# Layer 0 begun tile by tile: rows, turns, copies and first products of a bidirectional encoder trunk

## The reference, cut to what matters

```python
def rms_norm(x, g):
    y = x32 * lax.rsqrt(jnp.mean(x32 * x32, axis=-1, keepdims=True) + NORM_EPS)
    return (y * g)

for l in range(DEPTH):                                   # DEPTH = 2
    h = rms_norm(x, attn_pre_norm[l])
    proj = jnp.einsum('bsd,dc->bsc', h, w_in[l])         # 1024 -> IN_COLS
    gates, mla_in, dil_in, diff_in = jnp.split(proj, SPLITS, axis=-1)
    ...                                                  # three attention mixers
    merged = g_mla * (o_mla @ w_branch_mla[l]) + g_dil * (o_dil @ w_branch_dil[l]) + g_diff * (o_diff @ w_branch_diff[l])
    x = x + rms_norm(merged @ w_out[l], attn_post_norm[l])
    h = rms_norm(x, ffn_pre_norm[l])
    x = x + rms_norm(conv_gated_mlp(h, w_up[l], ffn_conv[l], w_down[l]), ffn_post_norm[l])
```

## Time and profile before

| | us |
|---|---|
| median of 3 runs | 1029.82 |
| lowest and highest | 1029.73, 1029.85 |
| the profiled execution | 1029.86 |
| its span | 1028.1 |
| TensorE busy in it | 1013.2 (99%) |
| VectorE busy | 680.5 (66%) |
| ScalarE busy | 587.8 (57%) |

### The profile page before, as it was taken

How to read it: one execution, slowest core, us unless ns; L and a number is a source line. 1 busy time by engine, 2 the same in 40 slices (tenths; PEclk the granted TensorE clock), 3 DMA queues, 4 the chain that set the end, 5 groups by cost and what they waited for, 6 DMA issues and landing times.

```text
span 1028.1 us, 15935 instructions
## 1 busy us (share of the span) xinstructions
PE 1013.2 (99%) x6244; PEld 908.7 (88%) x6244; DVE 680.5 (66%) x932; ACT 587.8 (57%) x859; POOL 131.9 (13%) x257
## 2 busy tenths in 40 slices
PE   8999999999999999999999999999999999999997
PEld 7889999888888999999888899998888889999996
DVE  5635566655596887878865355666555869787877
ACT  5657666565446654555575666565653457455553
POOL 3353124000002000000024321230000020000000
PEclk9999999999999999999999999999999999999999
DMA  8555445454444555565564544465344645546551
GB/s 253 184 172 158 123 136 172 162 165 164 144 147 160 202 169 203 168 201 173 166 195 155 173 124 126 150 207 164 124 139 168 205 144 166 204 169 201 174 195 41
DMA packets 109038, 170.79 MB, mean 166 GB/s; under 512 B 3377, under 2 KB 72804, under 8 KB 108964
## 3 DMA queue, kind: packets, MB, share of 16 engines
q1 hardware_dynamic: 107676, 166.88, 50.0%
q10 hardware_dynamic: 1208, 2.63, 0.7%
q0 software_dynamic: 80, 0.26, 0.1%
HBM read 168.72 MB, written 1.05 MB: 165 GB/s over the span
## 4 chain that ended last, share of the span: by engine, by line
PE 96%; DVE 1%; ACT 1%; issue 1%; DVEq 0%; POOL 0%; POOLq 0%; ACTq 0%
PE bank L1418 28%; PE bank L1420 28%; PE bank L1419 28%; PE bank L1781 2%; PE bank L1682 1%; PE bank L1703 1%; PE bank L1774 1%; PE bank L1691 1%; PE bank L1719 1%; PE bank L1726 1%; PE bank L1771 1%; PE bank L1733 1%; PE bank L1739 1%; PE bank L1397 0%; DVE x_rows L1233 0%
## 5 line engine op out<-in xcount | busy, mean ns | idle before, releaser
L1053 DVE TENSOR_TENSOR w_lo<-w_raw,w_hi 128x2048 fp32r<-128x2048 f32 (+3 forms) x174 | 364.3, 2095 | 161.1 <-ACT w_hi L700 161.0
L700 ACT ACTIVATE w_hi<-w_raw 128x2048 fp32r<-128x2048 f32 (+3 forms) x174 | 304.7, 1752 | 50.6 <-PE bank L1420 48.9
L1418 PE MATMUL bank<-w_hi,hT_lo 128*128 128x512 f32 (+2 forms) x700 | 258.3, 369 | 2.1 <-DVE hT_lo L1127 1.3
L1420 PE MATMUL bank<-w_hi,hT_hi 128*128 128x512 f32 (+2 forms) x700 | 252.9, 361 | 0.0
L1419 PE MATMUL bank<-w_lo,hT_hi 128*128 128x512 f32 (+2 forms) x700 | 252.6, 361 | 0.0
L1418 PE MATMUL bank<-hT_hi,w_lo 128*128 128x256 f32 x704 | 199.4, 283 | 0.7 <-DVE hT_lo L1080 0.7
L1420 PE MATMUL bank<-hT_hi,w_hi 128*128 128x256 f32 x704 | 199.2, 283 | 0.0
L1419 PE MATMUL bank<-hT_lo,w_hi 128*128 128x256 f32 x704 | 199.2, 283 | 0.0
L1418 PEld LDWEIGHTS bank<-w_hi,hT_lo 128*128 128x128 f32 x700 | 131.5, 188 | 18.3 <-issue 3.5
L1420 PEld LDWEIGHTS bank<-w_hi,hT_hi 128*128 128x128 f32 x700 | 131.4, 188 | 14.0
L1419 PEld LDWEIGHTS bank<-w_lo,hT_hi 128*128 128x128 f32 x700 | 131.7, 188 | 13.0
(11 more groups left out here) (215 smaller groups left out, 1250.9 us busy)
## 6 DMA issues: line engine op xcount, KB each, us to landing
w_raw<-in_w_up_dram SPq DMA_DIRECT2D x44, 1024.0 KB, 4.9
w_raw<-in_w_in_dram SPq DMA_DIRECT2D x36, 1024.0 KB, 5.0
w_raw<-in_w_in_dram SPq DMA_DIRECT2D x36, 768.0 KB, 4.3
w_raw<-in_w_down_dram SPq DMA_DIRECT2D x22, 1024.0 KB, 4.8
w_raw<-in_w_out_dram SPq DMA_DIRECT2D x8, 1024.0 KB, 4.9
w_raw<-in_w_in_dram SPq DMA_DIRECT2D x8, 672.0 KB, 4.1
w_raw<-in_w_branch_mla_dram SPq DMA_DIRECT2D x4, 1024.0 KB, 4.9
w_raw<-in_w_branch_diff_dram SPq DMA_DIRECT2D x4, 1024.0 KB, 5.0
```

The source lines that it names most:

```text
L700: nc.scalar.activation(w_hi[:, n % RING, 0:nk * cols], raw[:, n % RING, 0:nk * cols], ACT.Copy).then_inc(hi_done, 1)
L1053: V.tensor_tensor(w_lo[:, n % RING, s], raw[:, n % RING, s], w_hi[:, n % RING, s].bitcast(F32), ALU.subtract).then_inc(lo_done, 1)
L1418: PE.matmul(dst, lhs[1], rhs_hi, start=start, stop=False)
L1420: return PE.matmul(dst, lhs[0], rhs_hi, start=False, stop=stop)
```

## The change

SP's first DMAs come in another order: the two row blocks of tile 0, piece 0, the two blocks of tile 1, piece 1, piece 2. `x_landed` becomes one semaphore per tile. TensorE's layer 0 goes through `begin` as layer 1 does, with a branch of its own: turn tile 0 when its rows are in, turn tile 1 when its rows are in, products of tile 0 with piece 0 (`first_part`, high weights first), tile 1 with piece 0, tile 0 with piece 1, tile 1 with piece 1. `use_first` and the layer-0 branches of `empty_turn` go. ScalarE has `start_hi`: four pairs of tile 0, high half of piece 0, two pairs of tile 1, high half of piece 1, two pairs of tile 1. VectorE has `start_lo` in the same order. The squares of the rows stay behind it.

```diff
--- before.py
+++ after.py
@@ -422,7 +422,7 @@
         conv_mid, conv_done = sem("conv_mid"), sem("conv_done")
         gelu_done, g_ready, g_hi_done, g_lo_done = sem("gelu_done"), sem("g_ready"), sem("g_hi_done"), sem("g_lo_done")
         gain_landed = sem("gain_landed")
-        x_landed = sem("x_landed")
+        x_landed = [sem(f"x_landed{t}") for t in range(NT)]
         positions_landed, parameters_landed, par_turned = sem("positions_landed"), sem("parameters_landed"), sem("par_turned")
         attn_gain_landed = sem("attn_gain_landed")
         lambda_landed = sem("lambda_landed")
@@ -529,9 +529,12 @@
         @block.sync
         def _(sp):
 
-            for t in range(NT):
+            def load_x(t):
+
                 for h in range(2):
-                    sp.dma_start(x[64 * h:64 * h + 64, t, :], tokens[h, :, t, :]).then_inc(x_landed, 16)
+                    sp.dma_start(x[64 * h:64 * h + 64, t, :], tokens[h, :, t, :]).then_inc(x_landed[t], 16)
+
+            load_x(0)
             for l in range(DEPTH):
                 for n, piece in enumerate(PIECES):
 
@@ -544,6 +547,8 @@
                         sp.dma_start(par_rows[:, 0:3 * DEPTH, :],
                                      a["ffn_conv"].rearrange("l t (c p) -> c (l t) p", p=P)).then_inc(parameters_landed, 16)
 
+                    if l == 0 and n == 1:
+                        load_x(1)
                     sp.sem_inc(slot_claimed, 1)
                     sp.dma_start(cut(raw, n), weight_source(l, *piece)).then_inc(raw_landed[n % RING], 16)
             store_rows(sp, 0)
@@ -782,16 +787,10 @@
 
             def empty_turn(l, what, banks=slice(None)):
 
-                if what == "attn" and l == 0:
-                    act.wait_ge(par_ready, 1)
                 if what == "latent" and l == 0:
                     act.wait_ge(par_ready, 2)
                 for b, (k0, nk) in list(enumerate(TURN_BANKS[what]))[banks]:
                     m = TURN_BEFORE[what] + TURN_STEP[what] * (b + 1)
-                    if what == "attn" and l == 0 and b == 1:
-                        split_hi(l, 0)
-                    if what == "attn" and l == 0 and b == 3:
-                        split_hi(l, 1)
                     act.wait_ge(turn_full, l * NTURN + m)
                     src = bank[4 + b]
                     if what == "merged":
@@ -822,6 +821,15 @@
                                                     scale=par_all[:, l, PRE_A + k:PRE_A + k + 1])
                     last.then_inc(turn_hi, 1)
 
+            def start_hi():
+
+                act.wait_ge(par_ready, 1)
+                begin_hi(0, 0, range(4))
+                split_hi(0, 0)
+                begin_hi(0, 1, (0, 1))
+                split_hi(0, 1)
+                begin_hi(0, 1, (2, 3))
+
             def gated_hi(l, u):
 
                 act.wait_ge(g_ready, l * NU + (u + 1))
@@ -833,7 +841,8 @@
             def pre_attn(l):
 
 
-                act.wait_ge(x_landed, 16 * 4)
+                for landed in x_landed:
+                    act.wait_ge(landed, 16 * 2)
                 act.wait_ge(x_ready, X_START + l * 8)
                 for t in range(NT):
                     last = nc.scalar.activation(xn[:, t, :], x[:, t, :], ACT.Square, scale=1.0 / 32, accum_out=ss[:, 2 * t:2 * t + 1])
@@ -866,8 +875,10 @@
                         act.dma_start(post_gain[:], a["attn_post_norm"][l, :].partition_broadcast(P)).then_inc(gain_landed, 16)
                         if l == 0:
                             lambda_exps()
-                    elif what == "turn" and (l == 0 or step[1] != "attn"):
+                    elif what == "turn" and step[1] != "attn":
                         empty_turn(l, step[1])
+                    elif what == "turn" and l == 0:
+                        start_hi()
                     elif what == "mid":
                         post_square(l, 0, 0, 1)
                         pre_square(l, 0)
@@ -1055,10 +1066,6 @@
             def empty_turn(l, what, banks=slice(None)):
                 for b, (k0, nk) in list(enumerate(TURN_BANKS[what]))[banks]:
                     m = TURN_BEFORE[what] + TURN_STEP[what] * (b + 1)
-                    if what == "attn" and l == 0 and b == 1:
-                        split_lo(l, 0)
-                    if what == "attn" and l == 0 and b == 3:
-                        split_lo(l, 1)
                     dve.wait_ge(turn_hi, l * NTURN + m)
                     src = bank[4 + b]
                     if what == "merged":
@@ -1127,6 +1134,14 @@
                         last = V.scalar_tensor_tensor(out=hT_lo[:, k, cols], in0=begun_bank(t, k), scalar=par_all[:, l, PRE_A + k:PRE_A + k + 1],
                                                       in1=hT_hi[:, k, cols].bitcast(F32), op0=ALU.mult, op1=ALU.subtract)
                     last.then_inc(turn_emptied, 1)
+
+            def start_lo():
+
+                begin_lo(0, 0, range(4))
+                split_lo(0, 0)
+                begin_lo(0, 1, (0, 1))
+                split_lo(0, 1)
+                begin_lo(0, 1, (2, 3))
 
             def negmax_of(l, p):
 
@@ -1268,8 +1283,10 @@
                     elif what == "lambda" and l == 0:
                         lambda_sums()
                         lambda_parameters()
-                    elif what == "turn" and (l == 0 or step[1] != "attn"):
+                    elif what == "turn" and step[1] != "attn":
                         empty_turn(l, step[1])
+                    elif what == "turn" and l == 0:
+                        start_lo()
                     elif what == "mid":
                         for t in range(NT):
 
@@ -1446,32 +1463,6 @@
                 kk = k + 3 if kind == "ukv" else k
                 pe.wait_ge(turn_emptied, l * NTURN + (TURN_BEFORE[what] + TURN_STEP[what] * (kk // 2 + 1)))
 
-            def use_first(n):
-
-                hi, lo = cut(w_hi, n), cut(w_lo, n)
-                k0, cols = PIECES[n][2], PIECES[n][4]
-                left = [(k0 + k, t) for k in range(4) for t in range(NT)]
-                if n == 0:
-
-                    pe.wait_ge(hi_done, 1)
-                    for kk, t in left[0:4]:
-                        wait_turned(0, "mla", 0, kk)
-                        a_hi, a_lo = rows(hT_hi, hT_lo, kk, t)
-                        PE.matmul(bank[t][:, 0:cols], a_lo, hi[:, kk, :], start=kk == 0, stop=False)
-                        PE.matmul(bank[t][:, 0:cols], a_hi, hi[:, kk, :], start=False, stop=False)
-                    pe.wait_ge(lo_done, 1 + RING)
-                    for kk, t in left[0:4]:
-                        PE.matmul(bank[t][:, 0:cols], hT_hi[:, kk, t * P:(t + 1) * P], lo[:, kk, :], start=False, stop=False)
-                    left = left[4:]
-                else:
-                    pe.wait_ge(lo_done, n + 1 + RING)
-                for kk, t in left:
-                    wait_turned(0, "mla", 0, kk)
-                    last = passes(bank[t][:, 0:cols], rows(hT_hi, hT_lo, kk, t), hi[:, kk - k0, :], lo[:, kk - k0, :], False, kk == 7)
-                    if (kk, t) == (7, 0):
-                        last.then_inc(tile_full, 1)
-                last.then_inc(piece_used, 1)
-
             def turn_roots(l):
 
                 pe.wait_ge(root_rows_ready, l * NT + NT)
@@ -1481,8 +1472,6 @@
 
             def use_piece(l, n):
                 if n < 2:
-                    if l == 0:
-                        use_first(n)
                     return
                 kind, c, k0, nk, cols = PIECES[n]
                 if n in JOINED:
@@ -1558,7 +1547,9 @@
                 def turn_x(t):
 
                     for k in range(KD):
-                        if k % 4 == 0:
+                        if l == 0 and k == 0:
+                            pe.wait_ge(x_landed[t], 16 * 2)
+                        elif l and k % 4 == 0:
                             pe.wait_ge(x_ready, l * 8 + (2 * t + k // 4 + 1))
                         if t == 1 and k in (4, 6):
                             pe.wait_ge(turn_emptied, l * NTURN + (k // 2 - 2 + 1))
@@ -1571,7 +1562,7 @@
                     hi, lo = cut(w_hi, n), cut(w_lo, n)
                     k0, cols = PIECES[n][2], PIECES[n][4]
                     pe.wait_ge(lo_done, l * NPIECE + (n + 1 + RING))
-                    if n == 0:
+                    if l and n == 0:
                         pe.wait_ge(tile_emptied_dve, BASE + l * N_DVE - 3 + t)
                     for k in range(4):
                         if k % 2 == 0:
@@ -1579,6 +1570,29 @@
                         last = passes(bank[t][:, 0:cols], rows(hT_hi, hT_lo, k0 + k, t), hi[:, k, :], lo[:, k, :], k0 + k == 0, k0 + k == 7)
                     return last
 
+                def first_part():
+
+                    hi, lo = cut(w_hi, 0), cut(w_lo, 0)
+                    cols = PIECES[0][4]
+                    pe.wait_ge(hi_done, 1)
+                    for k in range(4):
+                        if k % 2 == 0:
+                            pe.wait_ge(turn_emptied, k // 2 + 1)
```

(17 more changed lines are left out.)

## The result

The changed kernel is slower: 1032.7 us (median of 20 runs, 1029.9 to 1033.92), the kernel before 1029.89 (20 runs, 1029.53 to 1031.15). The ratio is 1.0026, 95% interval 1.002 to 1.0032. The forecast was 1029.3, range 1028.6 to 1030.4. The single runs also spread more, over 4.0 us against 1.6.

What follows compares the result with a forecast made beforehand. It took the start of layer 0 to be bound by ScalarE's queue from 9.09 to 16.59 us, then VectorE's to 27.9. S of 11.73 gave a shift of -0.54: 1029.82 - 0.54 = 1029.3 us, range 1028.6 to 1030.4.

Steps and rivals of the forecast that it cites:

- The shift is S - 12.28: ScalarE's squares start at S + 2.23 against 14.51 today; that shift, -0.54 us, was let travel to the end.
- S: Start of ScalarE's high half of piece 1: latest of ScalarE itself (11.3), tile 1's rows, and piece 1; forecast 11.73 us.
- I take 9.9: Landing of tile 1's rows behind piece 0, from equal bytes ahead: 9.9 us, four ScalarE copies done by 11.4.
- the third, piece 1 at 11.7: Landing of piece 1, with the same blocks and piece ahead of it as today: 3.98 + 7.7 = 11.7 us.
- piece 0 at 7.3: Landing of piece 0 after tile 0's rows: 5.5 + 1.8 = 7.3 us, well before ScalarE needs it at 9.0.
- some 3 us before their bytes move at the least, so none is late: SP's DMA issues keep their number and 0.45 to 0.65 us each, some 3 us ahead of their bytes.
- The rival of late rows: Late tile 1 or piece 1 holds ScalarE's queue: halfway 1030.6 us, far end S = 14.4 and 1032.0; chance 0.14.
- The clock was taken as a case of its own: Rival: TensorE's clock falls in the 2.35 us gap after tile 0's turn; end -0.1, 1029.7 us; chance 0.08.
- the 0.64 us at piece 4: TensorE's wait for VectorE's low half before the product at 27.94; said to cover the loss from a fallen clock.
- an idle 1.70 us is harmless: In the earlier trace, products after TensorE's 1.70 us gap ran at full pace, so that gap did not lower the clock.
- the cost of the narrow copies: ScalarE's 16 copies of 128x128 at 0.254 us replace 8 of 128x256 at 0.36: 1.2 us more.
- nothing behind 28 us absorbs or adds much: After 27.4 us engines and the weights' ring are chained to one another, so the -0.54 us shift reaches the end.

Runs made afterwards that it cites:

- e5: Changed kernel with each tile's rows in one DMA over all 128 partitions, read from every second row of x (output not the reference's): 1029.44 us.
- e15: Changed kernel with each tile's rows over all 128 partitions in two DMAs of 256 KB, 512 columns each (output not the reference's): 1029.73 us.
- e2: Changed kernel with the DMAs in the order of the kernel before (four row blocks first), tile by tile work kept: 1029.72 us.
- e7: Changed kernel with second-half row blocks issued by ScalarE on its own queue, and SP's row blocks of both tiles ahead of the weights: 1030.75 us.
- e4: Changed kernel with each row block read from 64 neighbouring rows of x instead of every fourth (output not the reference's): 1032.07 us.
- e6: Changed kernel with second-half row blocks issued by ScalarE on its own queue, the first half's left where they are on SP's: 1029.66 us.
- e1: Changed kernel with 44 idle transposes of the identity between TensorE's turns of tile 0 and tile 1: 1031.98 us.
- e12: Changed kernel with the products of tile 0 with the first half of piece 0 put between the turns of tile 0 and tile 1: 1034.89 us.
- e14: Changed kernel with both tiles' rows first, halves of piece 2 ahead of the squares, and the masks' classes at VectorE's start: 1029.43 us.

## Why the prediction was wrong

- **The formula held.** "The shift is S - 12.28" gives 14.51 - 12.28 = +2.23, and both the squares and VectorE moved by 2.22 and 2.23. It holds beyond this run. S, the start of the high half of piece 1, can be read in the trace of every kernel with the new copies, and 1029.86 + S - 12.28 be set beside the time of the same profiled execution:

| | tile 1 complete | S | by the formula | measured | lowest clock from 8 to 20 us |
|---|---|---|---|---|---|
| e5 | 8.9 | 12.01 | 1029.59 | 1029.52 | 1.00 |
| e15 | 10.2 | 12.05 | 1029.63 | 1029.57 | 1.00 |
| e2 | 8.4 | 12.07 | 1029.65 | 1029.54 | 1.00 |
| e7 | 10.0 | 12.59 | 1030.17 | 1030.03 | 0.50 |
| e4 | 11.4 | 13.15 | 1030.73 | 1030.89 | 0.50 |
| e6 | 9.6 | 13.28 | 1030.86 | 1030.92 | 1.00 |
| changed kernel | 12.7 | 14.51 | 1032.09 | 1032.97 | 0.50 |
| e1 | 12.0 | 14.55 | 1032.13 | 1032.02 | 1.00 |
| e12 | 12.8 | 17.38 | 1034.96 | 1034.97 | 0.50 |

Eight of nine lie within 0.16 us of it. Only the changed kernel is off, by 0.9 us, its lateness at piece 4 by the clock. In e12 the clock fell too, but TensorE was waiting for VectorE again before piece 4 (33.03, wait 0.67). So ScalarE's queue decides, as the prediction had it, and the fallen clock cost time at the end only where TensorE had no wait left to cover it.

- **The step that failed is what S is made of**: the second of its three terms, "I take 9.9" for the rows of tile 1, and with it the third, piece 1 at 11.7, and piece 0 at 7.3. It held that the same bytes ahead take the same time. They took 12.7, 14.2 and 10.0; either of the first two alone puts S past 14. The row blocks alone had been slow (256 KB every 1.1 to 1.6 us) and the weights alone fast (379 GB/s), both in the earlier trace rows, and I let the slow part keep its length when it was put between the weights. It made the weights beside it slow as well: 156 to 225 GB/s from 7 to 12 us. The statement that SP's issues come "some 3 us before their bytes move at the least, so none is late" was wrong too: between tile 0's rows and piece 0 the DMA engines were half idle for a microsecond in the profiled execution (share 0.55; 0.80 in e1).
- **The rival of late rows was the case that came**, with the right mechanism and the right place. Its far end (tile 1 at 12.6, piece 1 at 14.4, S = 14.4, 1032.0) is nearly what happened; I gave the rival 0.14 and drew the range to less than half of it. The range should have reached 1032.0, since the trace of before had no row in which rows and weights were mixed.
- **The clock was taken as a case of its own**, covered by the 0.64 us at piece 4, with an idle 2.35 us. Late rows made the idle time 5.4 us, so the two came together, and as TensorE came later (3.1) than VectorE (2.23), the cover was used up: 0.9 us by the trace, 0.7 by e1. That an idle 1.70 us is harmless, as I read from one trace, is not safe either: in e14 the clock fell around gaps of 1.0 and 1.9 us, in e7 after one of 2.5, while in e15 it stayed through 2.8.
- **Right**: the first turn (6.29 against 6.5), ScalarE's start (6.78 against 7.0), tile 0 done at 8.8 (9.0), the cost of the narrow copies (0.25 us each), and that nothing behind 28 us absorbs or adds much (the span is 2.9 longer, TensorE 3.1 later at piece 4).
- A slower time beyond 0.2% had a chance of 0.03. The measured ratio, 1.0026 (1.002 to 1.0032), is there.

## What to carry to other kernels

Before a transfer is moved between others, ask for a row in which the two kinds run mixed; if there is none, bound its landing by the slowest rate seen for either, and let the range reach that. A queue of DMAs isn't paid by bytes alone: in this kernel, blocks that fill half of the partitions held the weights beside them to some 220 GB/s, where weights alone ran at 380. Find the one queue whose shift reaches the end (here ScalarE's, read at one row) and check it in every trace. And where a move makes one engine wait longer for a transfer, price the wait and the fallen clock together, and look at what stands in that engine's queue before filling the gap with work.

## What the runs showed of the hardware

- Row blocks of 256 KB on 64 partitions held the DMA engines at 156 to 225 GB/s from 7 to 12 us with pieces of weights beside them; from 7 to 9 us it was 221, against 338 and 292 with rows on 128 partitions (e5, e15). From 2 to 4 us, when the rows of tile 0 had the queue almost to themselves, there was no such difference: 252 in the changed kernel, 224 in e5 and 234 in e15.
- Transposes alone kept TensorE at the upper clock: 44 of them, 0.11 us apart, bridged 8.3 to 13.3 us in e1, and the granted clock stayed 1.00. The rule of the Trainium skill weighed in the prediction ("TensorE: Matmul & The Clock Gate", Part 4), by which transposes don't count as activity, does not hold in this kernel.
- The pace of TensorE rises at different times in different executions of like kernels: the 14 second warm-up transposes took 1.91 us before, and 2.85 in e1, where they stayed longer at 0.23 us apart. The column of the granted clock reads 1.00 there all the same; that the slow pace is the lower clock is taken from the turns of tile 1, which ran at that pace (8 in 1.97 us) at a granted 0.50. The first copies of ScalarE move with it by up to 1 us (6.78 in the changed kernel, 7.92 in e1).
- Once down, the clock stayed at 0.50 through the turns and products from 12.77 in the changed kernel, and was up again at 18.2.
